# The last stage of a transformer kernel with tokens instead of features on the partitions

## The reference

```python
def rmsnorm(x, g):
    y = x * lax.rsqrt(jnp.mean(x * x, axis=-1, keepdims=True) + NORM_EPS)
    return y * g

    x = x + jnp.square(jax.nn.relu(h @ w_ff1[i])) @ w_ff2[i]
    gate_p = jax.nn.sigmoid(rmsnorm(x, norm_ple_g[i]) @ w_ple_gate[i])
    x = x + gate_p * (p[i] @ w_ple[i])
    return rmsnorm(x, final_norm_g)
```

## Time and profile before

| | us |
|---|---|
| median of 3 runs | 1036.31 (1036.24 to 1038.28) |
| the profiled execution, its own time | 1037.56 |
| its span, first to last instruction | 1035.8 |
| around the span (1037.56 - 1035.8) | 1.76 |
| TensorE matmul busy | 993.6 (96%) |
| TensorE weight load busy | 962.9 (93%) |
| VectorE (DVE) busy | 761.8 (74%) |
| ScalarE (ACT) busy | 528.8 (51%) |
| mean granted TensorE clock, share of full | 0.992 |

### The profile page before, as it was taken

One profiled execution on the slowest core, in us unless ns is written; L12 is line 12 of the kernel. 1 busy time (PEld: TensorE's weight loads), 2 busy tenths in 40 slices (PEclk: granted clock), 3 DMA queues, 4 the chain that ended last, 5 costly groups with the idle time before them and its releaser, 6 DMA issues.

```text
span 1035.8 us, 18934 instructions
## 1 busy us (share of the span) xinstructions
PE 993.6 (96%) x7848; PEld 962.9 (93%) x7848; DVE 761.8 (74%) x1399; ACT 528.8 (51%) x911; POOL 10.5 (1%) x32
## 2 busy tenths in 40 slices
PE   4999999998898999999999999999899999999996
PEld 3999999997887999999999988799799999999996
DVE  6999998778976888685766598547578765565675
ACT  4455544435476555353655455654355554355443
POOL 0000000003000000000000000000000000000000
PEclk9999999999999999999999999999899999999998
DMA  8996999764573655688664446356455555555411
GB/s 317 357 337 260 363 337 332 295 206 141 202 267 100 219 193 191 218 232 248 222 241 164 163 135 228 125 160 182 123 188 169 188 185 174 193 193 206 151 62 41
DMA packets 34532, 215.09 MB, mean 208 GB/s; under 512 B 3725, under 2 KB 7693, under 8 KB 9614
## 3 DMA queue, kind: packets, MB, share of 16 engines
q1 hardware_dynamic: 34446, 213.88, 60.1%
HBM read 211.25 MB, written 2.62 MB: 206 GB/s over the span
## 4 chain that ended last, share of the span: by engine, by line
PE 82%; DVE 8%; ACT 4%; DMA 3%; issue 2%; POOL 1%; SPq 0%; DVEq 0%; ACTq 0%; POOLq 0%
PE bank L210 81%; DVE sb_ring L189 2%; DMA R<-scratch 2%; PE bank L213 1%; ACT sb_ring L186 1%; DMA sb_raw<-wts 1%; ACT sb_tmp L186 1%; DVE sb_tmp L198 1%; DVE sb_tq L189 1%; ACT R L186 1%; DVE sb_tmp L189 1%; DVE sb_junk L198 1%; DVE sb_tmp L192 0%; DVE sb_tmp L195 0%; POOL sb_st_a L189 0%
## 5 line engine op out<-in xcount | busy, mean ns | idle before, releaser
L210 PE MATMUL bank<-sb_h,sb_ring 128*128 128x256 f32 (+2 forms) x4224 | 522.5, 284 | 9.1 <-DVE sb_ring L189 4.1
L210 PEld LDWEIGHTS bank<-sb_h,sb_ring 128*128 128x128 f32 (+1 forms) x4224 | 512.7, 190 | 11.9 <-issue 5.5
L189 DVE TENSOR_TENSOR sb_ring<-sb_raw,sb_ring 128x1024 fp32r<-128x1024 f32 x322 | 384.7, 1210 | 3.0 <-ACT sb_ring L186 3.0
L186 ACT ACTIVATE sb_ring<-sb_raw 128x1024 fp32r<-128x1024 f32 x322 | 319.8, 1042 | 114.1 <-PE bank L210 62.3
L210 PE MATMUL bank<-R_512r,sb_ring 128*128 128x256 f32 x1920 | 235.5, 283 | 0.0
L210 PEld LDWEIGHTS bank<-R_512r,sb_ring 128*128 128x128 f32 x1920 | 232.0, 189 | 0.5 <-issue 0.3
L189 DVE TENSOR_TENSOR sb_tq<-bank,sb_rbc 128x256 f32<-128x256 f32 x107 | 42.9, 420 | 88.5 <-PE bank L210 47.9
L198 DVE CUSTOM_DVE_ANT_0 sb_junk<-sb_raw,sb_csil,sb_cols 128x1024 bf16<-128x1024 f32 x72 | 92.2, 1281 | 2.2 <-DMA sb_raw<-wts 0.4
L210 PE MATMUL bank<-R_1024r,sb_ring 128*128 128x256 f32 x768 | 91.5, 281 | 0.0
L210 PEld LDWEIGHTS bank<-R_1024r,sb_ring 128*128 128x128 f32 x768 | 91.3, 188 | 0.0
L210 PE MATMUL bank<-sb_ring,sb_h 128*128 128x512 f32 (+1 forms) x384 | 89.8, 387 | 0.0
(11 more groups left out here) (148 smaller groups left out, 524.9 us busy)
## 6 DMA issues: line engine op xcount, KB each, us to landing
sb_raw<-wts SPq DMA_DIRECT2D x194, 1024.0 KB, 5.0
R<-scratch SPq DMA_DIRECT2D x4, 768.0 KB, 8.5
scratch<-R SPq DMA_DIRECT2D x1, 1536.0 KB
sb_x<-xt SPq DMA_DIRECT2D x2, 512.0 KB, 5.1
out<-R SPq DMA_DIRECT2D x2, 512.0 KB, 2.9
sb_raw<-wts SPq DMA_DIRECT2D x1, 768.0 KB, 4.2
sb_raw<-wts SPq DMA_DIRECT2D x1, 640.0 KB, 4.0
sb_raw<-wts SPq DMA_DIRECT2D x1, 512.0 KB, 3.6
```

The lines of the kernel that those rows point to most:

```text
L186: return Issued(self.e and self.e.activation(o, i, func, **kw))
L189: return Issued(self.e and self.e.tensor_tensor(*a))
L210: return Issued(self.e and self.e.matmul(o, w, m, start=start, stop=stop, skip_group_check=True))
```

## The change

In the second half of the MLP, TensorE turns each finished tile of x to token-major with two transposes, one tile late (`turn_x`, into banks 4 to 7); `down_3` keeps to banks 0 to 3. Behind tile 3 and behind tile 7, ScalarE squares each turned bank with its row sum (`x_square`) and copies it to SBUF (`x_out`). The squares of the feature-major tiles, their sum in `acc`, the token sums, diagonals, `spread` and `rbc` of both last norms, and `turn_out` go away. The factor of the PLE norm becomes a scale of a partition (`ple_factor`), applied in the tanh.

The products of the last stage have h (128 tokens) stationary and the weights moving, 512 columns wide for `embed`, `embed_gate` and the first `last_gate`, 256 for the last two. The weights are six units now, of 1024, 2048 and 2048 columns for each half of the columns, and not five of 2048. The list `PLE_PARTS` gives the five parts of the output (token half t, columns a to b, slot of the sum). Parts 0 and 1 are the lower 512 columns of both token halves; part 2 is the upper columns of t=0, parts 3 and 4 are those of t=1. Each part goes through `ple_tanh`, `ple_gated`, `residual_4`, `final_square` and, but for parts 3 and 4, `final_scaled` with the gain row. The token half 0 gets its factor, its scaling and its store first. The gain is a row of 1024 broadcast to 128 partitions by one more DMA behind `load_p`.

```diff
@@ -101,8 +101,8 @@
         for f in range(0, 16, 2):
             ws += [("w", [tile("ff1", k, 16 * half + f + i) for k in range(8) for i in range(2)])]
         ws += chunks(down("ff2", 16, 16 * half))
-    ws += chunks([t for f in range(8) for t in [tile("wple", k, f) for k in range(2)]
-                  + [tile("wpg", k, f) for k in range(8)]])
+    for a in (0, 512):
+        ws += [("w", [("wple", k, a, a + 512) for k in range(2)])] + nat("wpg", [(a, a + 512)])
...
+PLE_PARTS = [(0, 0, 512, 2), (1, 0, 512, 2), (0, 512, 1024, 3), (1, 512, 768, 3), (1, 768, 1024, 4)]
...
@@ -1182,7 +1194,7 @@
                     self.add("p_lo")
                 if half == 0 and f == 2:
                     self.norm_rows(norm, FN.Square)
-            for f, bank in self.down(half, bk, 16, "down_3"):
+            for f, bank in self.down(half, Ring(m.banks[0:4]) if half else bk, 16, "down_3"):
                 q = tq.take()
                 self.add("down_scaled", half, f, bank, q)
                 done(bank, ("down_scaled", half, f))
@@ -1191,67 +1203,78 @@
                 if half:
                     self.hold = f >= 6
                     self.hx("pl", f)
-                    self.square("pl", f)
...
+                    if f == 1:
+                        self.x_banks = [b.take() for b in m.banks[4:8]]
+                    if f:
+                        self.turn_x(f - 1)
+
+    def turn_x(self, f):
+
+        for t in range(2):
+            self.add("turn_x", f, t, self.x_banks[f // 4 * 2 + t])
+        if f % 4 == 3:
+            for t in range(2):
+                b = self.x_banks[f // 4 * 2 + t]
+                self.add("x_square", t, f // 4, b)
+                self.add("x_out", t, f // 4, b)
+                done(b, ("x_out", t, f // 4), ("x_square", t, f // 4))
...
     def ple(self):
         m = self.m
-        B, tq = m.banks, m.tq
-        bk = Ring(B[0:4])
-        turned = [[B[4].take(), B[5].take()], [B[6].take(), None]]
+        B, tmp = m.banks, m.tmp
+
+        def embed(c):
+            banks = [b.take() for b in (B[0:2], B[4:6])[c]]
+            for k in range(2):
+                self.mm(512, "embed", c, k, banks)
+            return banks
+
+        def gated(n, e_bank, g_bank):
+            q = tmp.take()
+            self.add("ple_tanh", n, g_bank, q)
+            self.add("ple_gated", n, e_bank, q)
+            self.add("residual_4", n, q)
+            done(q, ("residual_4", n))
+
+        first = embed(0)
+        self.turn_x(NF - 1)
+        self.add("ple_factor")
         self.add("final_gain")
-
-        def product(f, between=None):
-            bank = bk.take()
-            for k in range(2):
-                self.mm(128, "embed", f, k, bank)
-            for k in range(8):
-                self.mm(128, "embed_gate", f, k, bank)
-                if between:
-                    between(k)
-            return bank
-
-        def gate(f, bank):
-            q = tq.take()
-            self.add("ple_in", f, bank, q)
-            self.add("ple_tanh", f, q)
-            return q
-
-        def evac(f, bank, q):
-            self.fill()
-            self.add("ple_gated", f, bank, q)
-            done(bank, ("ple_gated", f))
-            self.add("residual_4", f, q)
-            done(q, ("x", "pl", f))
-            self.square("fi", f)
-            self.add("final_scaled", f)
-
-        def turn(f):
-            for t in range(2):
-                self.add("turn_out", f, t, turned[f // 4][t])
-
-        first = product(0)
-        norm = self.x_norm("pl")
-        second = product(1)
-        third = product(2, lambda k: self.norm_rows(norm) if k == 0 else None)
-        firsts = [first, second, third]
-        gates = [gate(f, b) for f, b in enumerate(firsts)]
-        for f in range(3):
-            evac(f, firsts[f], gates[f])
-        for f in range(3, NF):
-            bank = product(f)
-            for i in ((), (0, 1, 2), (3,), (4,), (5,))[f - 3]:
-                turn(i)
-            evac(f, bank, gate(f, bank))
-            if f == 3:
-                bk = Ring(B[0:3])
-                turned[1][1] = B[3].take()
-        turn(6)
-        self.token_factor("fi")
-        turn(7)
-        for i in range(2):
-            self.add("final", i, turned)
-            self.add("store", i)
+        gates = [b.take() for b in B[2:4]]
+        for k in range(8):
+            self.mm(512, "embed_gate", k, gates)
+        for t in range(2):
+            gated(t, first[t], gates[t])
+            done(gates[t], ("ple_tanh", t))
+            self.add("final_square", t)
+            self.add("final_scaled", t)
+        second = embed(1)
+        gates = [b.take() for b in B[6:8] + B[2:3]]
+        self.need(U)
+        self.flush()
+        for k in range(8):
+            self.add("last_gate", 2, k, gates[0])
+        gated(2, second[0], gates[0])
+        self.add("final_square", 2)
+        self.add("final_scaled", 2)
+        for k in range(8):
+            self.add("last_gate", 3, k, gates[1])
+        gated(3, second[1], gates[1])
+        self.add("final_square", 3)
+        self.add("final_factor", 0)
+        for k in range(8):
+            self.add("last_gate", 4, k, gates[2])
+        gated(4, second[1], gates[2])
+        self.add("final", 0)
+        self.add("store", 0)
+        self.add("final_square", 4)
+        self.add("final_factor", 1)
+        self.add("final", 1)
+        self.add("store", 1)
+        self.went(U)
+        self.need(U)
+        self.went(U)
         self.add("end")
...
+        a, b = OR["fin_g"]
+        e.dma_start(m.fin_row(), m.rows_in[0:1, a:b].to_broadcast([128, 1024])).then_inc(
+            *self.up("gain_in", ("fin_row",), by=16))
...
     def store(self, i):
         m, e = self.m, self.e
         e.wait_ge(*self.at("final_low", i))
-        e.wait_ge(*self.at("final_high", i))
-        e.dma_start(m.out[i, :, :], m.reg(8 + 4 * i, 1024)).then_inc(*self.up(f"out{i}_out", ("out", i), by=16))
+        if i:
+            e.wait_ge(*self.at("final_high", i))
+        e.dma_start(m.out[i, :, :], m.result(i)).then_inc(*self.up(f"out{i}_out", ("out", i), by=16))
...
+    def last_gate(self, n, k, bank):
+
+        m, e = self.m, self.e
+        t, a, b, _ = PLE_PARTS[n]
         if k == 0:
             self.turn(bank)
-        e.wait_ge(*self.at("p_lo"))
-        ph, pl = m.p_pair()
-        self.tile(bank.ap[:, T:2 * T], (ph[:, T * k:T * k + T], pl[:, T * k:T * k + T]), k == 0, k == 1)
-
-    def embed_gate(self, f, k, bank):
-        e = self.e
-        e.wait_ge(*self.at("h", "pl", k))
-        self.tile(bank.ap[:, 0:T], self.m.hk(k), False, k == 7, *([("embed", f)] if k == 7 else []))
-
-    def turn_out(self, f, t, b):
+        w = self.w + k // 4
+        for part in range(2):
+            e.wait_ge(*self.at("lo", w, part))
+        c = 512 * (k % 4) + a - 512
+        ws = [m.ring[:, w % NS, i, c:c + b - a] for i in range(2)]
+        h = [x[:, 128 * t:128 * t + 128] for x in m.hk(k)]
+        ins = self.product(bank.ap[:, a - 512:b - 512], h, ws, k == 0, k == 7)
+        if k == 7:
+            ins.then_inc(*self.up("products", ("ple", n)))
...
+    def x_square(self, t, h, b):
+        m, e = self.m, self.e
+        e.wait_ge(*self.at("turn_x", 4 * h + 3, t))
+        if h:
+            e.wait_ge(*self.at("x_square", t, 0))
+        e.activation(m.junk[:, 512 * t:512 * t + 512], b.ap, FN.Square, accum_out=m.fst[:, t, h:h + 1]).then_inc(
+            *self.up("squares", ("x_square", t, h)))
+
+    def x_out(self, t, h, b):
+        m, e = self.m, self.e
+        e.activation(m.xn(t)[:, 512 * h:512 * h + 512], b.ap).then_inc(*self.up("x_out", ("x_out", t, h)))
+
+    def ple_tanh(self, n, bank, q):
+        m, e = self.m, self.e
+        t, a, b, _ = PLE_PARTS[n]
+        self.turn(q)
+        e.wait_ge(*self.at("ple_factor"))
+        e.wait_ge(*self.at("ple", n))
+        e.activation(q.ap[:, 0:b - a], bank.ap[:, a % 512:a % 512 + b - a], FN.Tanh, scale=m.fst[:, t, 6:7]).then_inc(
+            *self.up("gate_tanh", ("ple_tanh", n)))
+
+    def final_square(self, n):
+        m, e = self.m, self.e
+        t, a, b, c = PLE_PARTS[n]
+        e.wait_ge(*self.at("residual_4", n))
+        if n < 2:
+            e.wait_ge(*self.at("x_square", n, 1))
+        else:
+            e.wait_ge(*self.at("final_square", n - 2))
+        j = 512 * (n % 2)
+        e.activation(m.junk[:, j:j + b - a], m.xn(t)[:, a:b], FN.Square, accum_out=m.fst[:, t, c:c + 1]).then_inc(
+            *self.up("squares", ("final_square", n)))
+
+    def final(self, t):
+        m, e = self.m, self.e
+        n = 512 if t else 1024
+        e.wait_ge(*self.at("final_scaled", t))
+        if t == 0:
+            e.wait_ge(*self.at("final_scaled", 2))
+        e.wait_ge(*self.at("final_factor", t))
+        o = m.result(t)[:, 0:n]
+        e.activation(o, o, scale=m.nst[:, 1, t:t + 1]).then_inc(*self.up("final_low", ("final_low", t)))
...
+    def final_factor(self, t):
+        m, e = self.m, self.e
```

(118 more changed lines are left out.)

61 lines of the change are left out of this document (23 added, 38 removed).

## The result

The changed kernel takes 1038.47 us (median of 20 runs, 1036.41 to 1042.67); the kernel before, run beside it, 1036.40 us (20 runs, 1034.92 to 1039.08). The ratio is 1.0023, with a 95% interval of 1.0015 to 1.0031: slower by 2.07 us, or 0.2%. The time lies in the range, 1034.2 to 1039.0, and above the 1036.9 forecast for the likeliest case. That case had a clock that stays up; the first rival, a clock that falls behind the new stall, has come.

A forecast was written before the change was run, and what follows sets the result against it. TensorE was taken to bound everything but the tail. The last store's issue came +0.9 us later, less 0.3 for its landing: +0.6 in total, from 1036.3 to 1036.9 us; range 1034.2 to 1039.0.

The forecast's parts named there:

- the likeliest case: Whole kernel: a late-split stall of 2.6 us with the clock staying up, median 1036.9 us; chance 0.46.
- the first rival: Behind the last-stage stall: clock low for about 3 us of products, losing 1.4 to 1.6 us, result 1038.4; chance 0.26.
- The MLP half: MLP's second half on TensorE: six transpose pairs, 1.3 us, plus a 0.5 us stall, together 1.8 us added.
- the stall behind tile 1: MLP's second half: TensorE waits for x of tile 0 before its transposes, 0.5 us, bounds 0.3 and 0.7.
- The last stage to the lower products: Last stage on TensorE: transposes, embed(0) and embed_gate take 14.44 us; lower products seen at 1010.8.
- The new wait: Middle of part 2: TensorE stalls 2.6 us for the last weights' two split pieces, listed behind both gated parts.
- the path: Last stage, from lower products seen through both gated parts to the split pieces' end: 8.05 us, bounds 7.8 to 8.4.
- The tail: End of kernel, from last products seen to last scaling done: 5.4 us, where it was 6.5.
- R: TensorE's restart in the last stage, 8.05 us behind the lower products being seen; put at 1018.8.
- The stores: End of kernel: the last store no longer shares the DMA engines; 0.3 us less taken, between none and 0.6.
- The sum: Whole kernel: last store issued 0.9 us later, 0.3 off for its landing, total +0.6 us.
- its clock term: Last stage, products behind the stall: 1.5 us added to 1036.9 for a lowered clock, giving 1038.4.

The follow-up runs named there:

- e1: The changed kernel with the last unit's two split pieces listed before the first gated part; median 1033.91 us, ratio 0.9970 to the kernel before.
- e4: e1 with the transposes of tile 0 moved behind tile 2 of the MLP's second half; median 1033.47 us, ratio 0.9968 to the kernel before.
- e6: The changed kernel with both tanh ahead of the squares in ScalarE's list, split still late; median 1038.57 us, ratio 1.0012 to the kernel before.
- c4: The kernel of e6, unaltered, in a second profiled execution; length 88.83 us from the start of the MLP's second half.
- e2: The changed kernel with one of the two late split pieces put before the first gated part; median 1036.46 us, ratio 1.0001 to the kernel before.
- e5: The kernel before, its last unit's two split pieces held back until behind the residual of tile 5; median 1038.06 us, ratio 1.0015 to the kernel before.
- e3: e1 with the last square put before the scaling of the first token half on ScalarE; median 1032.93 us, ratio 0.9965 to the kernel before.
- c2: The changed kernel, unaltered, in a second profiled execution; time 1041.22 us, length 92.32 us from the start of the MLP's second half.
- c3: The changed kernel, unaltered, in a third profiled execution; time 1041.48 us, length 92.23 us from the start of the MLP's second half.

## Why the prediction was right or wrong

**The MLP half: right.** Up to and with the first pair behind it, 45.57 + 1.8 + 0.22 = 47.59 us were predicted, and 47.61 measured (946.81 to 994.42). A pair costs 0.21 us (a tile goes from 5.70 to 5.91). Of the stall behind tile 1 the bracket names 0.34, at the lower bound; but start to start it is more. In e1 the first product of tile 2 starts 12.08 us behind the start of the half (948.10 and 960.18). The 96 products before it take 96 x 0.1187 = 11.40 and the pair 0.21, which leaves 0.47 for the stall, near the 0.5 that was taken. The 0.54 us that e4 saves here (47.57 us in e1, 47.03 in e4) hold 0.07 more, because four transposes in a row take 0.35 us and not twice 0.21.

**The last stage to the lower products: right.** They were to be seen 62.0 us after the start of the half, and were after 62.10 (1008.91 - 946.81).

**The new wait: right in place and mechanism.** Predicted 2.6 us in the middle of part 2 for `sb_ring` of VectorE, measured 2.79; the path was to be 8.05 us and was 8.12 to the end of the second piece (1017.03), 8.27 to TensorE's next start. The terms that the prediction lists add up to 8.15, not 8.05. They hold two errors that nearly cancel. I took 0.03 us for each handoff, which is what the tiny operations of the tail show, but a VectorE step of 512 that needs the one before it starts 0.79 us behind it where the step takes 0.69, so 0.10. On the other side, steps that don't need the one before them overlap it: the second tanh starts 0.63 us behind the square (0.72 and a handoff were taken), the first piece 0.61 behind `final_scaled`. TensorE's restart comes 0.15 us behind the second piece. The strict order of the queues ("TensorE: Matmul & The Clock Gate", section "Architectural detail: the array is 16x 32x32, not 1x 128x128", in the Trainium skill) is borne out by this case's runs: e1 and e6 change nothing but the order, and the wait goes to nothing and to 2.14 us.

**The clock: the step that failed.** The likeliest case left the clock at 1.00 behind the stall, since the engine is dense on both sides of it. That argument did not hold in the profiles of after: the clock fell while TensorE still waited, with dense work before and behind. The rival was given 0.26, and its price was too small for these executions as well. That the length of the stall alone decides is not borne out either: at 2.14 us the clock fell once and stayed up once. I took one spell of about 3 us from the earlier trace rows and a loss of 1.4 to 1.6. A low stretch of 3.4 us does cost that (1.60, e6 against c4), but after shows a low stretch of 6.8 us, twice as long as that one. From TensorE's restart to the end of the last scaling, it takes 17.06 us in after and 14.26 in c4, where 14.05 was predicted: 2.8 us for the clock. The Trainium skill ("TensorE: Matmul & The Clock Gate", section "HAM oscillation — how this bites in real kernels") has idle gaps followed by matmuls at the low clock. The rows of after agree, with products at 0.50 behind 2.79 us; those of c4, e2 and e5, at 1.00 behind 2.14, 2.03 and 1.44 us, do not show it.

**The tail: right in time, with another step in its chain.** From the last products seen (1028.70) to the last scaling done (1034.24) it is 5.5 us, predicted 5.4. The prediction's list of the chain was first factor, part 4, last square, second factor. In the chain that ended last, the last square waits not for part 4 but for the first half's scaling, which stands ahead of it in ScalarE's list:

```profile
1029.71 0.04 ACT R L188
1029.76 1.01 issue
1030.77 0.50 ACT sb_junk L188 x2
1031.27 0.03 issue
```

The square's input was there at 1030.38, and it started at 1030.77. The prediction's working did have the square start behind that scaling, at R + 10.7, so the sum was not hurt; e3 takes the wait away.

**The stores: the bound was the value.** The prediction read the earlier trace rows as 3.2 us for the first store and 2.6 for the second, and took 0.3 off for a lone one. In after the two are issued 3.4 us apart, and each takes 2.6:

```profile
L218 SPq DMA_DIRECT2D out<-R x2: 338/343/348, 1030.9 to 1034.3; - x2
...
DMA to landing us min/median/max: 2.6/2.6/2.6
```

The span ends 0.5 us behind that landing (1034.3 + 2.6 = 1036.9 of 1037.4). With the same 0.5 in before, the last landing was at 1035.3 and the 3.2 belong to the second store: the change saves 0.6 there, not 0.3. That is inferred from the ends of the spans. The estimate of 3.2 us for a lone store, worked out in the prediction from the Trainium skill ("DMA: Bandwidth & Descriptors", section "Anatomy of one DMA"), is not what this store takes.

**The sum.** By lengths, after minus before is 3.57 us. The prediction has +0.6; to it come 2.8 for the clock, 0.1 up to the lower products, 0.2 for the path to TensorE's restart and 0.2 from there to the last scaling, and 0.3 go off for the store. Without the fall, c4's stages and the stall of after, 88.83 + 0.65 = 89.5 us, would stand 0.7 above before. So the terms added up, and the chance was put on a case that none of the three profiles of after shows. That the rival's 1038.4 is nearly the median of 1038.47 is partly luck: its clock term was 1.5 where the profiles have 2.8. The median's +2.07 is less than the length's +3.57. By the estimate above, from the 20 times and clocks, at least part of that is executions with a shorter low stretch or none. Starts of the half that differ between the runs can add to it; how much each gives is not shown.

**Open:** what decides whether the clock falls. It fell in waits of 2.79, 2.80, 2.80 and 2.14 us, and not in 2.14, 2.03 and 1.44. In the four that fell it did so when TensorE had been idle for 2.0 to 2.2 us (cut finer, the granted clock falls at 1016.53 in after, 1018.59 in c2, 1018.77 in c3 and 1017.75 in e6), in e6 only 0.05 us before the restart; c4, with the same wait as e6, stayed at 1.00. Also open are the 0.37 us of VectorE in e2, and whether the gains of e3 and e4 reach the median.

## What to carry to other kernels

When steps are regrouped into wider ones, look at what was queued between the old ones: here two pieces of weight splitting had their place between small steps, and lost it, and one line that drains them ahead of the first waiting step turned a loss of 0.2% into a gain of 0.3%. Price a TensorE stall of the size seen here, 2 to 3 us, twice, once as it is and once with the clock down behind it, and give the second real odds even where the engine is dense on both sides. Where the upstream part varies by more than the edit gives, compare the profiles' lengths from a fixed point before the edit, and let the medians decide only what they can.

## What the runs showed of the hardware

- The clock fell inside a wait, not behind it: at about 1016.5 us in after, with TensorE idle since 1014.4 and busy without a gap since 958.7 before that.
- Low stretches came in two sizes, 3.4 us (e6) and 6.8 us (after, three times); nothing between was seen behind these stalls.
- At one and the same stall of 2.14 us the clock fell in one execution and not in the next, which made 1.6 us of length.
- A lone store of 512 KB took 2.6 us from issue to landing, also with the other issued 2.0 us ahead (e3); only with the two 0.6 us apart did one take 3.2.
- The idle time in a bracket understates a stall: start to start the losses were 2.93 for 2.79, 1.6 for 1.44 and 0.47 for 0.34.
